# Rows of 256 columns without gaps for the moving operands of a two-block float32 network

## The chip, the cores and the metric

The kernel runs on one core of one Trainium2 chip. The metric is the device time of one execution in microseconds; lower is better. TensorE does the matrix products, ScalarE (ACT) and VectorE (DVE) split numbers and evaluate the elementwise parts, GpSimd (POOL) helps them, and SyncE (SP) issues nearly all the weight loads.

## The reference

Two blocks of depth 2 on a model width of 1024. The first block puts 16 meta tokens ahead of the 256 tokens of the sequence and works on 272 tokens; its result without the meta tokens goes to the second block.

```
first block, for each layer l of 2:
    h = h + 0.5 * swiglu(rmsnorm(h))                # 1024 -> 2 x 2816 -> 1024
    h = h + concat(retention(...), diff_attention(...)) @ w_out
    h = h + 0.5 * swiglu(rmsnorm(h))
h = rmsnorm(h)[:, 16:]
second block, for each layer i of 2:
    h = h + 0.5 * swiglu(rmsnorm(h))
    h = h + (short_conv if i == 0 else dilated_attention)(rmsnorm(h))
    h = h + 0.5 * swiglu(rmsnorm(h))
```

All data is float32, and so is the result.

## The kernel before

**Layout.** Everything is kept transposed: the model dimension lies on the 128 partitions in `KC` = 8 chunks, the tokens lie along the columns. `T` is 272 (16 meta tokens, `META`, and 256 tokens, `SEQ`). The residual `h` has rows of 272 columns for the whole kernel.

**Two parts for every number.** A float32 factor is split into a high part (rounded to the type fp32r) and a low part (the rest). A product of two such numbers takes three terms: high weights with the high input, high weights with the low input, low weights with the high input. The input of a stage is in `x[partition, chunk, part, column]`, the gated products of a feed-forward stage are in `a`, with 22 chunks (`FCH`) in place of 8, and the mixed values of an attention stage of the first block are in `y`. In all three a row has 272 columns, the high row of a chunk is followed by its low row, and the low row by the high row of the next chunk.

```
x = alloc(ctx, [P, KC, 2, T], F32R)
a = alloc(region, [P, FCH, 2, T], F32R)
y = alloc(region, [P, KC, 2, T], F32R)
```

**Stages.** `STAGES` lists twelve of them: feed-forward, mixer, feed-forward, feed-forward on all 272 tokens; a mixer (stage 4) whose keys and values need all 272 but whose queries and output need only the 256; and from there on 256 tokens alone: feed-forward (5), feed-forward (6), convolution (7), feed-forward (8), feed-forward (9), dilated attention (10), feed-forward (11). A stage of 256 tokens uses columns 16 to 271 of `x` and of `y`, and columns 0 to 255 of `a`. So it leaves a gap of 16 columns (64 bytes) between the rows that it reads.

**TensorE's loop.** One output tile is 128 channels by all tokens of the stage, summed in one PSUM bank over 8 chunks (22 in the down projection of a feed-forward stage, 2 tiles at a time). For each chunk and tile `matmuls` issues the three terms as three matmuls (lines 1641, 1642, 1643). In the five feed-forward stages of 256 tokens (`joined`) the first two terms are one matmul of 512 columns (line 1639), whose moving operand is `both(k)`: the high row and the low row of a chunk, two runs of 256 columns. Its sums with the high and the low rows lie side by side in one bank and are added later by ACT and DVE. The last two tiles of each down projection go back to three matmuls (`halves`). The text calls the matmuls of one chunk and tile, 768 columns in all, a *group*: two matmuls where the first two terms are joined, three elsewhere.

```
if both is not None:
    pe.matmul(ps[:, r.banks[j], :].rearrange("p (m n) -> p m n", m=2), hi, both(k), start=i == 0, stop=False)
else:
    pe.matmul(o, hi, xhi, start=i == 0, stop=False)
    pe.matmul(o, hi, xlo, start=False, stop=False)
ins = pe.matmul(o, lo, xhi, start=False, stop=i == r.nk - 1)
```

**Other buffers of 256 tokens.** The convolution keeps its result in `c_yy` and the dilated attention in `d_y`. Both are `[P, KC, 2, SEQ]` already, with rows of 256 columns without gaps, and their output projections read them with three matmuls a group. In the dilated attention the values are projected the other way round (`values`, lines 1959 to 1961): `x` is stationary there, and the moving operand is three pieces of 128 columns of the weights. The norms of queries and keys (lines 1894, 1895) move the rows `d_sqh` and `d_sql` of 512 columns in one run.

**Who feeds TensorE.** SP loads weights in pieces of up to 1 MB into a ring of four (`raw`), waiting for the low parts that DVE makes. ACT makes the high part of the weights (line 810), DVE the low part (line 1135), seven tiles ahead at most. ACT writes the high rows of `x` (823), `a` (909, 946) and `y`, DVE the low rows of `x` (1148), DVE or POOL those of `a` (1266, 743), POOL those of `y`. TensorE waits for the low row of each chunk (`xl`, `al`, `yl_d`, `yl_r`).

## Time and profile before

| | us |
|---|---|
| median of 3 runs (2184.85 to 2186.58) | 2186.07 |
| span of the profiled execution | 2188.4 |
| TensorE busy in the span | 2173.7 (99%) |
| VectorE busy | 1559.0 (71%) |
| ScalarE busy | 1221.3 (56%) |
| GpSimd busy | 438.6 (20%) |

The profiled execution is 2188.4 us long from its first to its last instruction, and no other time of it is given; it stands 2.3 us above the median of the runs. Matmuls are pipelined: the duration of one in the profile (281 ns for 256 columns) runs past the start of the next, so what a matmul costs in a dense stretch is the distance from its start to the next start. That distance is read from the timeline, over many groups, since its times are rounded to 10 ns. Some matmul records are missing from the trace, so distances are counted in groups by the order in the code, not by counting rows.

### The profile page before, as it was taken

To read this page: it belongs to the slowest core of one execution; us is meant where nothing else is said; L and a number is where in the kernel's file an instruction comes from. 1 tells how busy PE (TensorE), PEld (TensorE's weight loads), DVE (VectorE), ACT (ScalarE), POOL (GpSimd) and SP (SyncE) were. 2 spreads that over 40 slices of the span, in tenths; PEclk is the share of its full clock that TensorE was granted. 3 is DMA by queue.
4 is the path that set the end of the run, shared out by engine and by line. 5 is a ranking of instruction groups with operands and counts; after the bars stand their busy time and mean duration, and the time that the engine had idled before them with its cause. 6 is when DMAs were issued, how large, how long until landed. Compare 5 with 4: busy or idle time off the path is not lost.

```text
span 2188.4 us, 38657 instructions
## 1 busy us (share of the span) xinstructions
PE 2173.7 (99%) x15616; PEld 2045.6 (93%) x15616; DVE 1559.0 (71%) x2589; ACT 1221.3 (56%) x2020; POOL 438.6 (20%) x468
## 2 busy tenths in 40 slices
PE   9999999999999999999999999999999999999999
PEld 9999999999999999888988999889888999999888
DVE  7655876765665586876697587865876688887863
ACT  6444465544544446665565444655655566676652
POOL 1000522420350142231053000430331000000420
PEclk9999999999999999999999999999999999999999
DMA  8555434975786543565465554655555566674653
GB/s 271 195 171 177 155 122 136 232 199 167 196 209 179 169 154 116 173 205 185 162 204 198 196 182 146 221 198 186 185 185 179 160 190 168 176 236 140 222 177 104
DMA packets 429264, 395.34 MB, mean 181 GB/s; under 512 B 16559, under 2 KB 426031, under 8 KB 429088
## 3 DMA queue, kind: packets, MB, share of 16 engines
q1 hardware_dynamic: 416464, 377.11, 54.7%
q0 software_dynamic: 12336, 15.51, 3.6%
q8 instruction: 124, 2.03, 0.4%
q14 instruction: 52, 0.43, 0.1%
q10 hardware_dynamic: 288, 0.27, 0.0%
HBM read 389.20 MB, written 7.41 MB: 181 GB/s over the span
## 4 chain that ended last, share of the span: by engine, by line
PE 91%; DVE 4%; ACT 2%; DMA 1%; issue 1%; SPq 0%; DVEq 0%; ACTq 0%
PE ps L1643 29%; PE ps L1639 25%; PE ps L1641 16%; PE ps L1642 15%; DVE t L1135 2%; PE ps L1961 1%; PE ps L1960 1%; PE ps L1959 1%; DMA t<-attn_w_qkv 1%; ACT t L968 0%; PE ps L1927 0%; ACT t L810 0%; PE ps L1940 0%; PE ps L1911 0%; DVE t L1347 0%
## 5 line engine op out<-in xcount | busy, mean ns | idle before, releaser
L1643 PE MATMUL ps<-t 128*128 128x256 f32 (+1 forms) x5504 | 1563.6, 284 | 0.0
L1643 PEld LDWEIGHTS ps<-t 128*128 128x128 f32 x5504 | 1039.4, 189 | 0.1
L1135 DVE TENSOR_TENSOR t<-t 128x1024 fp32r<-128x1024 f32 (+1 forms) x724 | 880.5, 1232 | 176.5 <-ACT t L810 176.0
L1641 PE MATMUL ps<-t 128*128 128x272 f32 (+1 forms) x3084 | 891.9, 289 | 2.4 <-DVE t L1598 2.4
L1642 PE MATMUL ps<-t 128*128 128x272 f32 (+1 forms) x3084 | 883.6, 287 | 0.0
L810 ACT ACTIVATE t<-t 128x1024 fp32r<-128x1024 f32 (+1 forms) x724 | 731.9, 1030 | 263.3 <-PE ps L1643 235.1
L1639 PE MATMUL ps<-t 128*128 128x512 f32 x2420 | 847.4, 394 | 0.0
L1641 PEld LDWEIGHTS ps<-t 128*128 128x128 f32 x3084 | 582.5, 189 | 8.8 <-issue 5.0
L1642 PEld LDWEIGHTS ps<-t 128*128 128x128 f32 x3084 | 584.5, 190 | 0.9
L1639 PEld LDWEIGHTS ps<-t 128*128 128x128 f32 x2420 | 454.4, 188 | 103.3 <-DVE t L1135 0.3
L750 POOL TENSOR_TENSOR t<-t 128x256 f32<-128x256 f32 x110 | 100.9, 917 | 734.3 <-ACT t L926 734.3
L916 ACT ACTIVATE t<-ps 128x256 f32<-128x256 f32 x220 | 83.1, 378 | 138.7 <-PE ps L1643 138.3
L773 POOL DMA_DIRECT2D bias_bands<-bias_rows x128 | 105.1, 829 | 216.5 <-PE ps L1643 164.1
L743 POOL TENSOR_TENSOR t<-t 128x256 fp32r<-128x256 f32 x110 | 126.7, 1152 | 9.5 <-ACT t L909 9.5
L823 ACT ACTIVATE t<-t 128x256 fp32r<-128x256 f32 (+1 forms) x96 | 50.0, 531 | 93.5 <-DVE t L1220 83.5
L946 ACT ACTIVATE t<-t 128x272 fp32r<-128x272 f32 x66 | 28.5, 432 | 117.0 <-DVE t L1315 117.0
L1170 DVE SCALAR_TENSOR_TENSOR t<-ps,t 128x512 f32<-128x512 f32 (+2 forms) x52 | 28.6, 551 | 83.6 <-ACT t L851 83.2
L1281 DVE TENSOR_TENSOR t<-ps,t 128x256 f32<-128x256 f32 x110 | 46.7, 425 | 52.1 <-ACT t L916 49.3
L909 ACT ACTIVATE t<-t 128x256 fp32r<-128x256 f32 x110 | 45.4, 413 | 65.3 <-DVE t L1285 65.3
L1274 DVE TENSOR_TENSOR t<-ps,t 128x256 f32<-128x256 f32 x110 | 46.2, 420 | 47.6 <-ACT t L916 47.1
L1285 DVE TENSOR_TENSOR t<-t 128x256 f32<-128x256 f32 x110 | 69.3, 630 | 0.0
L1312 DVE TENSOR_TENSOR t<-ps,t 128x272 f32<-128x272 f32 x66 | 29.0, 440 | 51.0 <-PE ps L1643 51.0
(197 smaller groups left out, 1503.1 us busy)
## 6 DMA issues: line engine op xcount, KB each, us to landing
t<-ffn_w_in SPq DMA_DIRECT2D x88, 1024.0 KB, 5.3
t<-ffn_w_gate SPq DMA_DIRECT2D x42, 1024.0 KB, 5.4
t<-ffn_w_up SPq DMA_DIRECT2D x42, 1024.0 KB, 6.7
t<-attn_w_qkv SPq DMA_DIRECT2D x72, 512.0 KB, 4.9
t<-ffn_w_down SPq DMA_DIRECT2D x32, 1024.0 KB, 5.2
t<-ffn_w_out SPq DMA_DIRECT2D x32, 1024.0 KB, 5.2
t<-w_in SPq DMA_DIRECT2D x28, 1024.0 KB, 5.0
t<-ffn_w_down SPq DMA_DIRECT2D x16, 768.0 KB, 4.4
```

Source lines behind the costliest of these rows:

```text
L743: pool.tensor_tensor(a[:, j, 1, 0:SEQ], us[:, j % 2, 0:SEQ], f32(a[:, j, 0, 0:SEQ]), ALU.subtract).then_inc(S["al"], 1)
L750: pool.tensor_tensor(sl[:, j % 2, 0:SEQ], sl[:, j % 2, 0:SEQ], rstd[:, META:T], ALU.mult).then_inc(S["factor"], 1)
L773: pool.dma_start(bands.ap()[n, 64 * r:64 * r + 64, q, c:end].rearrange("i (k j) -> k i j", j=64), bass.AP(scr, n * NSEG * P + seg * P + 63 ...
L810: act.activation(whi[:, plan.place[n], 0:nk, :], raw[:, u % NRAW, 0:nk, half * P:half * P + P], ACT.Copy).then_inc(S["hi"], 1)
L823: act.activation(placed(e, x[:, m, 0, c0:T]), hm, ACT.Copy, scale=gain(e, m)).then_inc(S["xh"], 1)
L916: act.activation(part[:, m, :], ps[:, plan.bank[t], SEQ:2 * SEQ], ACT.Copy).then_inc(S["part"], 1)
L1135: dve.tensor_tensor(wlo[:, plan.place[n], 0:nk, :], raw[:, u % NRAW, 0:nk, half * P:half * P + P], f32(whi[:, plan.place[n], 0:nk, :]), AL ...
L1285: dve.tensor_tensor(us[:, i, 0:N], us[:, i, 0:N], sl[:, i, 0:N], ALU.mult).then_inc(S["prod"], 1)
L1639: pe.matmul(ps[:, r.banks[j], :].rearrange("p (m n) -> p m n", m=2), hi, both(k), start=i == 0, stop=False)
L1641: pe.matmul(o, hi, xhi, start=i == 0, stop=False)
L1642: pe.matmul(o, hi, xlo, start=False, stop=False)
L1643: ins = pe.matmul(o, lo, xhi, start=False, stop=i == r.nk - 1)
```

## The change

`close(t, n)` gives a second view of the same memory: the first `n * 512` columns of the buffer as `n` chunks of two rows of 256 columns. `x_close`, `a_close` and `y_close` are these views of `x`, `a` and `y`. `parts_of(e)` gives for the input of stage `e` the old view where it has 272 tokens and the new one where it has 256 (stages 5 to 11); `products_of(s)` and `mixed_of(s)` do the same for `a` and `y`. Stages 0 to 4 keep their input in the old view, and stage 4 has its mixed values in the new one. Everything that writes or reads these buffers goes through the three functions. The number of instructions, their order, their engines, their sizes and the semaphores are those of before. No buffer is added or made smaller.

```diff
--- before.py
+++ after.py
@@ -545,6 +545,25 @@
         def f32(ap):
             return ap.bitcast(F32)
 
+        def close(t, n):
+
+            whole = t[:, :, :, :].rearrange("p k m c -> p (k m c)")
+            return whole[:, 0:n * 2 * SEQ].rearrange("p (k m c) -> p k m c", k=n, m=2)
+
+        x_close, a_close, y_close = close(x, KC), close(a, FCH), close(y, KC)
+
+        def parts_of(e):
+
+            return x if start_of(e) == 0 else x_close
+
+        def products_of(s):
+
+            return a if STAGES[s][1] == 0 else a_close
+
+        def mixed_of(s):
+
+            return y if STAGES[s][1] == 0 else y_close
+
         def gain(e, m):
 
             if e == FINAL:
@@ -715,8 +734,8 @@
 
                 def low_y(kind, i, c):
                     w.wait_ge(*of_head("yh", l, kind, i))
-                    pool.tensor_tensor(y[:, c, 1, cq:T], yv[:, cq:T] if kind == "d" else qk[:, i, cq:T],
-                                       f32(y[:, c, 0, cq:T]), ALU.subtract).then_inc(S["yl_" + kind], 1)
+                    hi, lo = (mixed_of(s)[:, c, m, 0:T - cq] for m in range(2))
+                    pool.tensor_tensor(lo, yv[:, cq:T] if kind == "d" else qk[:, i, cq:T], f32(hi), ALU.subtract).then_inc(S["yl_" + kind], 1)
 
                 def step(what, i):
                     if what == "O2":
@@ -740,7 +759,7 @@
 
                 def low_a(j):
                     w.wait_ge(S["ah"], FCH * f + j + 1)
-                    pool.tensor_tensor(a[:, j, 1, 0:SEQ], us[:, j % 2, 0:SEQ], f32(a[:, j, 0, 0:SEQ]),
+                    pool.tensor_tensor(a_close[:, j, 1, :], us[:, j % 2, 0:SEQ], f32(a_close[:, j, 0, :]),
                                        ALU.subtract).then_inc(S["al"], 1)
 
                 w.wait_ge(S["rstd"], s + 1)
@@ -820,7 +839,7 @@
                 hm = residual(e, m, c0)
                 sem, value = made(e, m)
                 w.wait_ge(sem, value)
-                act.activation(placed(e, x[:, m, 0, c0:T]), hm, ACT.Copy, scale=gain(e, m)).then_inc(S["xh"], 1)
+                act.activation(placed(e, parts_of(e)[:, m, 0, 0:T - c0]), hm, ACT.Copy, scale=gain(e, m)).then_inc(S["xh"], 1)
 
             def squared(e, m):
                 c0 = start_of(e)
@@ -906,7 +925,7 @@
 
                 def high_a(j):
                     w.wait_ge(S["prod"], FCH * f + j + 1)
-                    act.activation(a[:, j, 0, 0:N], us[:, j % 2, 0:N], ACT.Copy).then_inc(S["ah"], 1)
+                    act.activation(products_of(s)[:, j, 0, 0:N], us[:, j % 2, 0:N], ACT.Copy).then_inc(S["ah"], 1)
 
                 def second(j, m, t):
 
@@ -943,7 +962,7 @@
                     act.activation(sl[:, j % 2, 0:N], gs[:, j % 2, 0:N], ACT.Silu).then_inc(S["silu"], 1)
                     behind(T0[s] + 2 * j)
                     w.wait_ge(S["prod"], n)
-                    act.activation(a[:, j, 0, 0:N], us[:, j % 2, 0:N], ACT.Copy).then_inc(S["ah"], 1)
+                    act.activation(products_of(s)[:, j, 0, 0:N], us[:, j % 2, 0:N], ACT.Copy).then_inc(S["ah"], 1)
                     behind(T0[s] + 2 * j + 1)
                 if joined(s)[0]:
                     high_a(FCH - 1)
@@ -988,7 +1007,7 @@
                     root(ps[:, bank, 0:NQ], lanes[lane][2][:, 0:NQ], lanes[lane][1][:, 0:NQ], "hroot_" + kind)
 
                 def high_y(kind, i, c):
-                    act.activation(y[:, c, 0, cq:T], yv[:, cq:T] if kind == "d" else qk[:, i, cq:T], ACT.Copy).then_inc(S["yh_" + kind], 1)
+                    act.activation(mixed_of(s)[:, c, 0, 0:NQ], yv[:, cq:T] if kind == "d" else qk[:, i, cq:T], ACT.Copy).then_inc(S["yh_" + kind], 1)
 
                 def step(what, i):
                     if what == "D1":
@@ -1145,8 +1164,8 @@
                 sem, value = made(e, m)
                 w.wait_ge(sem, value)
                 w.wait_ge(S["xh"], KC * e + m + 1)
-                dve.scalar_tensor_tensor(placed(e, x[:, m, 1, c0:T]), hm, gain(e, m), placed(e, f32(x[:, m, 0, c0:T])),
-                                         ALU.mult, ALU.subtract).then_inc(S["xl"], 1)
+                hi, lo = (parts_of(e)[:, m, i, 0:T - c0] for i in range(2))
+                dve.scalar_tensor_tensor(placed(e, lo), hm, gain(e, m), placed(e, f32(hi)), ALU.mult, ALU.subtract).then_inc(S["xl"], 1)
 
             def added(e, m):
                 c0 = start_of(e)
@@ -1263,7 +1282,7 @@
 
                 def low_a(j):
                     w.wait_ge(S["ah"], FCH * f + j + 1)
-                    dve.tensor_tensor(a[:, j, 1, 0:N], us[:, j % 2, 0:N], f32(a[:, j, 0, 0:N]),
+                    dve.tensor_tensor(products_of(s)[:, j, 1, 0:N], us[:, j % 2, 0:N], f32(products_of(s)[:, j, 0, 0:N]),
                                       ALU.subtract).then_inc(S["al"], 1)
 
                 def both_parts(j, n, t, i):
@@ -1650,8 +1669,9 @@
                     if r.piece == 0:
 
                         w.wait_ge(*((S["lo_first"], k + 1) if k < KC - 1 else (S["lo"], 4)))
-                matmuls(r, range(KC), lambda k, c0: (x[:, k, 0, c0:T], x[:, k, 1, c0:T]), ready, hook,
-                        both=(lambda k: x[:, k, :, META:T]) if STAGES[r.stage][0] == FFN and joined(r.stage)[0] else None)
+                xs, first = parts_of(r.stage), start_of(r.stage)
+                matmuls(r, range(KC), lambda k, c0: (xs[:, k, 0, c0 - first:T - first], xs[:, k, 1, c0 - first:T - first]), ready, hook,
+                        both=(lambda k: x_close[:, k, :, :]) if STAGES[r.stage][0] == FFN and joined(r.stage)[0] else None)
 
             def norm(e):
                 c0 = start_of(e)
@@ -1699,8 +1719,8 @@
                     w.wait_ge(S["al"], FCH * f + k + 1)
                 for r in runs:
                     if r.first - T0[s] >= 2 * FCH:
-                        matmuls(r, range(FCH), lambda k, c0: (a[:, k, 0, 0:N], a[:, k, 1, 0:N]), ready,
-                                both=(lambda k: a[:, k, :, 0:N]) if halves(s, r) else None)
+                        matmuls(r, range(FCH), lambda k, c0: (products_of(s)[:, k, 0, 0:N], products_of(s)[:, k, 1, 0:N]), ready,
+                                both=(lambda k: a_close[:, k, :, :]) if halves(s, r) else None)
 
             def start_work():
                 w.wait_ge(S["squares"], 64)
@@ -1862,7 +1882,7 @@
                         w.wait_ge(*of_head("hn", l, "r", 3))
                     if m in (6, 7):
                         w.wait_ge(*of_head("hn", l, "d", 3))
-                    matmuls(r, OUT_ORDER, lambda k, c0: (y[:, k, 0, c0:T], y[:, k, 1, c0:T]), ready, each=each if m == 0 else None)
+                    matmuls(r, OUT_ORDER, lambda k, c0: (mixed_of(s)[:, k, 0, 0:NQ], mixed_of(s)[:, k, 1, 0:NQ]), ready, each=each if m == 0 else None)
 
             def conv(s):
                 runs = plan.runs[s]
@@ -1954,7 +1974,7 @@
                         w.wait_ge(S["evac"], plan.earlier[r.first + j] + 1)
                         for k in range(KC):
                             hook[j](k)
-                            xhi, xlo = (x[:, k, m, META + j * P:META + (j + 1) * P] for m in range(2))
+                            xhi, xlo = (x_close[:, k, m, j * P:(j + 1) * P] for m in range(2))
                             hi, lo = (wt[:, p0:p0 + 3, k, :] for wt in (whi, wlo))
                             pe.matmul(o, xhi, hi, start=k == 0, stop=False)
                             pe.matmul(o, xhi, lo, start=False, stop=False)
```

## Rows read from the trace of the kernel before

**Rows 1.** The page: engines, clock in 40 slices, chain that ended last.

```profile
PE 2173.7 (99%) x15616; PEld 2045.6 (93%) x15616; DVE 1559.0 (71%) x2589; ACT 1221.3 (56%) x2020; POOL 438.6 (20%) x468
...
PEclk9999999999999999999999999999999999999999
...
PE 91%; DVE 4%; ACT 2%; DMA 1%; issue 1%; SPq 0%; DVEq 0%; ACTq 0%
```

**Rows 2.** Waits of TensorE: engine line, for whom, us in total, times, longest.

```profile
PE ps L1940 <- ACT t L1082: 2.6, 1, 2.6
PE ps L1641 <- DVE t L1598: 2.4, 2, 1.9
```

**Rows 3.** Busy time by stretch: window, us, then each engine; last clock, DMA share, GB/s.

```profile
1100.00:1200.00 100.00, 100.00 (x574) 87.84 (x573) 84.90 (x123) 62.59 (x115) 45.02 (x40) 1.00 0.64 211
1275.00:1330.00 55.00, 55.00 (x466) 55.00 (x465) 48.73 (x84) 23.19 (x28) 0.00 (x0) 1.00 0.64 212
1790.00:1940.00 150.00, 150.00 (x1316) 144.36 (x1315) 126.53 (x228) 108.83 (x170) 4.75 (x9) 1.00 0.68 190
```

**Rows 4.** Groups by line and form, TensorE: count | busy us, mean ns | idle.

```profile
L1643 PE MATMUL ps<-t 128*128 128x256 f32 x3504 | 985.7, 281 | 0.0
L1639 PE MATMUL ps<-t 128*128 128x512 f32 x2420 | 847.4, 394 | 0.0
...
L1641 PE MATMUL ps<-t 128*128 128x256 f32 x1084 | 308.7, 285 | 0.0
```

**Rows 5.** Timeline, TensorE, up projection of stage 5: start us, duration us.

```profile
1001.18 0.39 PE L1639 MATMUL ps<-t 128*128 128x512 f32 x1
1001.42 0.28 PE L1643 MATMUL ps<-t 128*128 128x256 f32 x1
...
1008.88 0.39 PE L1639 MATMUL ps<-t 128*128 128x512 f32 x1
```

**Rows 6.** Timeline, TensorE, down projection of stage 6, joined groups.

```profile
1230.26 0.39 PE L1639 MATMUL ps<-t 128*128 128x512 f32 x1
...
1237.92 0.39 PE L1639 MATMUL ps<-t 128*128 128x512 f32 x1
```

**Rows 7.** Timeline, TensorE, down projection of stage 6, last two tiles.

```profile
1254.90 0.29 PE L1641 MATMUL ps<-t 128*128 128x256 f32 x1
...
1263.76 0.28 PE L1641 MATMUL ps<-t 128*128 128x256 f32 x1
```

**Rows 8.** Timeline, TensorE, projections of stage 7 from `x`.

```profile
1299.97 0.28 PE L1641 MATMUL ps<-t 128*128 128x256 f32 x1
...
1300.33 0.28 PE L1641 MATMUL ps<-t 128*128 128x256 f32 x1
...
1300.68 0.28 PE L1641 MATMUL ps<-t 128*128 128x256 f32 x1
...
1307.81 0.28 PE L1641 MATMUL ps<-t 128*128 128x256 f32 x1
```

**Rows 9.** Timeline, TensorE, output projection of stage 7 from `c_yy`.

```profile
1337.90 0.28 PE L1641 MATMUL ps<-t 128*128 128x256 f32 x1
...
1344.90 0.28 PE L1641 MATMUL ps<-t 128*128 128x256 f32 x1
```

**Rows 10.** Timeline, TensorE, projections of stage 10 from `x`.

```profile
1819.03 0.28 PE L1641 MATMUL ps<-t 128*128 128x256 f32 x1
...
1824.01 0.28 PE L1641 MATMUL ps<-t 128*128 128x256 f32 x1
```

**Rows 11.** Timeline, TensorE, values and norms of stage 10.

```profile
1837.92 0.39 PE L1894 MATMUL ps<-t 128*128 128x512 f32 x1
1838.15 0.39 PE L1895 MATMUL ps<-t 128*128 128x512 f32 x1
1838.38 0.34 PE L1959 MATMUL ps<-t 128*128 128x384 f32 x1
...
1843.07 0.40 PE L1894 MATMUL ps<-t 128*128 128x512 f32 x1
```

## The prediction, made before the changed kernel was run

> **What bounds the kernel now.** I read the page first: TensorE is busy for 99% of the span, its clock is granted in full in all 40 slices, and 91% of the chain that ended last is TensorE's own [rows 1]. Then TensorE's waits: the longest is 2.6 us, the next 2.4 us in sum [rows 2], so nothing feeds it late. Then stretches inside the stages that the change touches: in a feed-forward stage, the convolution and the dilated attention TensorE is never idle, the clock is 1.00, and the next engine, DVE, is busy for 84.9, 88.6 and 84.4% [rows 3]. The kernel's time is the sum of the distances between matmul starts. The change adds and removes no instruction. It can change the time only if these distances depend on where the rows of the moving operand lie. That is the one question, and the timeline answers part of it.
>
> **The distances now.** All are of a group: one chunk, one tile, 768 columns.
> - Joined, from `x`: 22 groups between 1001.18 and 1008.88, so 350.0 ns [rows 5].
> - Joined, from `a`: 22 groups between 1230.26 and 1237.92, so 348.2 ns [rows 6].
> - Three matmuls, from `a`: 25 groups between 1254.90 and 1263.76, so 354.4 ns [rows 7].
> - Three matmuls, from `x`, convolution: 22 groups between 1299.97 and 1307.81, so 356.4 ns. They alternate between about 0.36 and 0.35 us, with even and odd chunks [rows 8].
> - The same in the dilated attention: 14 groups between 1819.03 and 1824.01, so 355.7 ns [rows 10].
> - Three matmuls from `c_yy`, whose rows have no gaps: 20 groups between 1337.90 and 1344.90, so 350.0 ns [rows 9].
>
> The last two kinds differ in nothing but the buffer: same three terms, same 256 columns, same clock, same engine busy without a pause. With gaps a group costs 6.4 ns (1.8%) more than without. That the distance alternates with the parity of the chunk fits: with gaps a chunk is 2176 bytes, so the starting place of its rows within any larger block of memory differs from chunk to chunk, and in `c_yy`, at 2048 bytes a chunk, it does not.
>
> **What the groups become.** The number of groups follows from the loops and agrees with the counts by form [rows 4]. Up projections: 5 stages x 44 tiles x 8 chunks = 1760 joined groups. Down projections: 5 x 6 x 22 = 660 joined (together the 2420 of line 1639) and 5 x 2 x 22 = 220 of three matmuls. Convolution: 24 x 8 = 192. Dilated attention, queries and keys: 48 x 8 = 384. Output of stage 4: 8 x 8 = 64. The remaining 224 of the 1084 groups of line 1641 are the output projections from `c_yy` and `d_y` (128) and the queries and gates of stage 4 (96), whose `x` stays as it is.
>
> Groups of three matmuls: the nearest row is `c_yy`, and I take its 350.0 ns. That gives 220 x 4.4 = 1.0 us, 192 x 6.4 = 1.2 us, 384 x 5.7 = 2.2 us, and for the 64 of stage 4, which I cost like those from `a`, 64 x 4.4 = 0.3 us. Sum 4.7 us. Bounds: nothing (the address has another effect than I think), and the 4.7 us in full plus as much again as 348 ns instead of 350 would give, 860 x 2 = 1.7 us, so 6.4 us.
>
> Joined groups: no row shows 512 columns of a joined group without the gap. Three rows are near. The values of the dilated attention move 384 columns of the weights in runs that have no odd offsets: 27 matmuls in the 4.69 us between 1838.38 and 1843.07, so 173.7 ns each, 0.452 ns per column [rows 11]. `c_yy` gives 116.7 / 256 = 0.456 ns. The norms move 512 columns in one run: two distances, 0.46 us together, 230 ns or 0.449 ns per column [rows 11]; these were short stretches, read to 10 ns. For 768 columns this makes 347.4, 350.0 and 345.0 ns. The joined groups from `a` stand at 348.2 already, though they have the gap, so part of what a gap costs is gone where two rows are read in one instruction. I take 348.0 ns for both kinds: 1760 x 2.0 = 3.5 us and 660 x 0.2 = 0.1 us. Bounds: nothing if they stay as they are, and with 345.0 ns, 1760 x 5.0 + 660 x 3.2 = 10.9 us.
>
> **A rule weighed.** Rows 11 and 5 show 0.23 us for 512 columns in one run and 0.24 us for 512 in two runs with a gap between. The Trainium skill (Advanced Engine Details and Errata, Memory Cachelines) says that any non-contiguous access pattern slows down matmuls significantly; it says so of PSUM, and if it held for the moving operand too, joining two runs into one would be worth much more than my 3.6 us. The trace doesn't bear this out: by the two rows the difference is 10 ns at most, and by the groups 5 ns.
>
> **The rest of the change at nothing.** ACT, DVE and POOL write the same numbers of elements into rows that start elsewhere, with unit steps as before. These writes lie beside TensorE, which waits for none of them now, and in the tightest stretch, the convolution, DVE still has 11% of its time free [rows 3]. If TensorE gets 1.8% faster there, DVE's share goes from 88.6 to 90.2%, and it stays covered. Were the cover gone, the cost would be the lateness of `xl` or `al` at a chunk, of which there is none now beyond [rows 2]. The values in stage 10 only load their stationary operand from the new view; the moving one is the weights, so their 173.7 ns stay. No buffer is shared by two stages at once in a new way: the input of a stage is written after the projections of the one before are done, and no wait is added. Transfers follow DVE and find the same ring, and they are busy for 0.64 to 0.68 of the time [rows 3]; 0.4% more is no strain.
>
> **The sum.** 4.7 + 3.6 = 8.3 us of the profiled 2188.4, so a span near 2180.1. The profile stands 2.3 us above the median of the runs, and the saving is the same there: 2186.1 - 8.3 = 2177.8 us, 0.38% faster. About 0.2%, 4.4 us, is what a measurement of this kernel can tell from no change.
>
> **The rivals.**
> - *Only groups of three gain.* The joined ones read two rows in one instruction, and the gap between them may cost nothing, as the 350.0 of `x` joined equals the 350.0 of `c_yy`. Against it stands `a` joined at 348.2 with another start of its rows: the start matters in joined groups too. Time 2186.1 - 4.7 = 2181.4.
> - *Nothing changes.* The 6.4 ns of the convolution would then come from something else that differs between its projections and its output, such as DVE and ACT, which work harder in the projections. For it: I have compared stretches, not the same stretch twice. Against it: the distances repeat with the parity of the chunk, which the work of DVE doesn't. Time 2186.1. The Trainium skill (TensorE: Matmul & The Clock Gate, Back-to-back issue gap) gives columns / 2.4 GHz + 2.5 ns from start to start, in which no address stands; by that rule a joined group is 325 ns now and after. The trace has 350, so the rule lacks the very part that is in question here.
> - *The joined groups gain all that the bound allows*: 2186.1 - 4.7 - 10.9 = 2170.5.
> - *Slower: every row starts at the bad place.* In the convolution groups of one parity take about 0.35 and of the other 0.36 us [rows 8]; as 356.4 is their mean, the slow ones take some 362 ns if the fast ones take what `c_yy` does. After the change all chunks of `x` and of `a` start at the same place within 1024 bytes, and high and low rows too. If this is the slow one, every group takes 362 ns: 1760 x 12 + 660 x 13.8 + 220 x 7.6 + 576 x 6.2 + 64 x 7.6 = 35.9 us more, 2222 us. It decides as soon as the changed groups average above the present mean, which is (1760 x 350.0 + 660 x 348.2 + 284 x 354.4 + 576 x 355.9) / 3280 = 351.1 ns. Against it: `c_yy`, `d_sqh` and the weights as moving operand, three buffers with equal starts for all rows, are all at or under 350.
>
> **How the numbers follow.** Forecast (both kinds gain, 6 to 12 us) 0.55; only groups of three 0.15; nothing 0.17; the largest gain 0.05; slower 0.08. Predicted 2177.8. The range leaves out the slower case and the far end of the largest gain: 2171.0 to 2186.3. The forecast's own range is 2174 to 2180. Faster by over 0.2%: 0.55 + 0.05, and 0.08 of the second case, which lies on the bound: 0.68. Within 0.2%: 0.17 + 0.07 = 0.24. Slower: 0.08.
>
> **What would show it.** In the timeline after, the projections of the convolution no longer alternate, and 22 groups take 7.70 us instead of 7.84 (step one). In the up projections 22 groups take 7.66 instead of 7.70, and 7.59 at the bound (step two). The down projections keep 7.66. The output of the convolution keeps 350.0. Stages 0 to 3 take the same time to within a microsecond. The waits of TensorE are as short as before. The prediction is wrong if the convolution stays at 356 (then the address was not the cause), or if the up projections rise above 351 ns a group.

## The result and the profile after

| | before | after |
|---|---|---|
| median of 9 runs each, us | 2185.34 (2183.92 to 2186.58) | 2188.70 (2186.32 to 2194.17) |
| span of the profiled execution | 2188.4 | 2187.9 |

The ratio is 1.0018, with a 95% interval of 1.0010 to 1.0025: the changed kernel is slower by 0.18%, which is within the 0.2% that the prediction called no change. The forecast was 2177.8 us, and the measured time lies above its range. The runs after lie 7.9 us apart, those before 2.7; but on the chip of the first experiments 15 runs of the kernel before lay 6.5 us apart (2184.21 to 2190.71), so such a spread is no mark of the change.

The page after (engines, chain), and TensorE's longest waits:

```profile
PE 2176.6 (99%) x15616; PEld 2043.4 (93%) x15616; DVE 1557.4 (71%) x2589; ACT 1222.2 (56%) x2020; POOL 441.5 (20%) x468
...
PE 93%; DVE 3%; ACT 2%; DMA 1%; issue 1%; SPq 0%; DVEq 0%; ACTq 0%
```

```profile
PE ps L1914 <- DVE t L1523: 2.0, 2, 1.1
PE ps L1960 <- ACT t L1101: 1.4, 1, 1.4
PE ps L1792 <- ACT t L1026: 1.4, 2, 0.8
```

As in [rows 1, 2] TensorE is the bound and hardly waits. So the answer is again in the distances. Timeline of TensorE after (start us, duration us), each pair of rows 22 groups apart: first the up projections of stage 5, then those of stage 6, then the last two tiles of stage 6's down projection, then the projections of the convolution from `x`:

```profile
950.26 0.40 PE L1658 MATMUL ps<-t 128*128 128x512 f32 x1
...
957.88 0.40 PE L1658 MATMUL ps<-t 128*128 128x512 f32 x1
...
1100.15 0.40 PE L1658 MATMUL ps<-t 128*128 128x512 f32 x1
...
1107.93 0.40 PE L1658 MATMUL ps<-t 128*128 128x512 f32 x1
...
1250.20 0.28 PE L1660 MATMUL ps<-t 128*128 128x256 f32 x1
...
1258.12 0.28 PE L1660 MATMUL ps<-t 128*128 128x256 f32 x1
...
1290.02 0.28 PE L1660 MATMUL ps<-t 128*128 128x256 f32 x1
...
1297.94 0.28 PE L1660 MATMUL ps<-t 128*128 128x256 f32 x1
```

Divided by 22 these are 346.4, 353.6, 360.0 and 360.0 ns a group, against 350.0 [rows 5], 354.4 [rows 7] and 356.4 [rows 8]. The groups of three from `x` and `a` are slower than before, and at exactly 120 ns a matmul they no longer alternate between chunks. The joined groups do what no step of the prediction allows for: with the same rows at the same places, stage 5 runs at 346.6 and stage 6 at 353.4. The means over the groups of a stage in the two traces, in ns (distances between neighbouring groups with no other matmul and no wait between them; in stages 7 and 10 the projections from `x`, in stage 4 the output from `y`), and how long each stage lasts, from its first norm matmul to the next stage's, in us:

| stage | 4 | 5 | 6 | 7 | 8 | 9 | 10 | 11 |
|---|---|---|---|---|---|---|---|---|
| joined, before | | 349.6 | 349.6 | | 349.6 | 349.6 | | 349.6 |
| joined, after | | 346.7 | 353.4 | | 347.1 | 353.3 | | 353.4 |
| of three, before | 355.2 | 354.9 | 354.9 | 356.1 | 354.9 | 354.9 | 355.5 | 354.9 |
| of three, after | 350.4 | 359.7 | 360.0 | 359.9 | 359.7 | 360.0 | 359.4 | 360.0 |
| lasts, before | 141.9 | 182.1 | 185.6 | 94.1 | 182.1 | 180.9 | 289.5 | 176.6 |
| lasts, after | 140.9 | 181.1 | 187.7 | 95.0 | 181.1 | 182.9 | 288.3 | 178.5 |

Stages 4 to 11 together last 2.6 us longer after. Stages 5 and 8 gain 1.0 us each, and 6, 9 and 11 lose 2.1, 2.0 and 1.9, each as its groups say (stage 6: 484 x 3.8 + 44 x 5.1 = 2.1 us). Stage 4 gains 0.3 us in its output, whose groups from `y` fell from 355.2 to 350.4 ns, and 0.5 in shorter waits. Stage 10 loses 1.5 us in its groups: once it is in its steady course, a pair of heads takes 31.69 us in place of 31.50. That it is 1.2 us shorter all the same has two causes that have nothing to do with its groups: its longest wait fell from 2.6 to 1.4 us, and in the trace of the kernel before TensorE had half its clock for 3.4 us, right behind that wait. Window, us, engines, then clock (0.50 is 1.2 GHz, 1.00 is 2.4), in the kernel before:

```profile
1764.00:1767.00 3.00, 0.37 (x5) 0.17 (x4) 1.45 (x2) 2.54 (x4) 0.00 (x0) 1.00 0.96 254
1767.40:1770.80 3.40, 3.40 (x31) 2.81 (x26) 2.28 (x4) 3.34 (x6) 0.00 (x0) 0.50 0.82 236
```

An estimate from its length and clock is that it costs 1.7 us, so at the full clock stages 4 to 11 would last 4.3 us longer after. Two more lie in stage 0 (from 12.96 and from 67.57 us, 3.4 us each), and the trace after has none: its mean granted clock is 1.000, against 0.998 before. That is why stages 0 to 3, which the change leaves alone, took 3.1 us less in it, and why the profiled span after is shorter than the one before. The medians of nine runs are the measure.

### The profile page after: what moved, and what is told of

It is laid out like the page before. It is cut to its first block, busy times and chain, and to the rows that moved or that the text cites. A ratio compares the mean times of both kernels' runs of the same rounds, so it can differ in the third digit from the quotient of the medians.

```text
span 2187.9 us, 38657 instructions
## 1 busy us (share of the span) xinstructions
PE 2176.6 (99%) x15616; PEld 2043.4 (93%) x15616; DVE 1557.4 (71%) x2589; ACT 1222.2 (56%) x2020; POOL 441.5 (20%) x468
## 4 chain that ended last, share of the span: by engine, by line
PE 93%; DVE 3%; ACT 2%; DMA 1%; issue 1%; SPq 0%; DVEq 0%; ACTq 0%
PE ps L1662 29%; PE ps L1658 26%; PE ps L1660 16%; PE ps L1661 16%; DVE t L1154 1%; PE ps L1981 1%; PE ps L1979 1%; PE ps L1980 1%; DMA t<-attn_w_qkv 1%; PE ps L1947 0%; ACT t L829 0%; PE ps L1931 0%; PE ps L1960 0%; PE ps L1757 0%; ACT t L866 0%
```

## The experiments

Two theories stood at the outset. *Address*: the distance is a function of where the rows start. *Rhythm*: rows that all start alike let the stream of matmuls fall into one of several self-repeating patterns, and one layout has several distances. A third was traffic of the other engines. All ratios are to the kernel before, run on the same chip; differences between two changed kernels in microseconds can be across chips.

**1. Streams of groups alone** (m1_streams). A kernel of its own, 1475.7 us long: no gating, no evacuation, nothing but matmuls in 32 stretches after the operands are loaded.

```
for seg, (kind, first, stride, low, tiles, pause) in enumerate(SEGMENTS):
    ...
    hi, lo = whi[:, n % NP, k, :], wlo[:, n % NP, k, :]
    ...
        pe.matmul(o, hi, xh, start=k == 0, stop=False)
        pe.matmul(o, hi, xl, start=False, stop=False)
    pe.matmul(o, lo, xh, start=False, stop=k == KC - 1)
```

> This kernel computes nothing of the reference: it loads four weight pieces, splits them, copies the input to both rows of x, and then runs 32 stretches of the group's matmuls with no other engine at work, most after a short pause; its output is the untouched input. It varies the layout of the moving rows (with gaps as in x and in a; without; without and shifted by 8, 16, 32 columns; gap only between chunks; gap only between high and low row), the kind of group (two or three matmuls), and what ran just ahead. Address theory (the distance is a function of where the rows start): each layout has one distance wherever it stands, three matmuls without gaps 359.8 ns, joined without gaps 347 or 353, and shifts of 8 to 32 columns move it. Rhythm theory (equal rows let the stream fall into one of several self-repeating rhythms, which lasts until something breaks it): the same joined stretch without gaps takes 346.7 in some places and 353.3 in others, depending on whether three-matmul groups or a pause came ahead; with gaps 350 always. Traffic theory (DVE, ACT or DMA traffic makes the difference): with these idle, all layouts take the same, near 347.

Its timeline, 22 groups apart: groups of three without gaps at a shift of 0, at a shift of 16 columns, then joined groups without gaps at a shift of 0 in two of the stretches:

```profile
130.31 0.28 PE L112 MATMUL ps<-t 128*128 128x256 f32 x1
...
138.23 0.28 PE L112 MATMUL ps<-t 128*128 128x256 f32 x1
...
225.05 0.28 PE L112 MATMUL ps<-t 128*128 128x256 f32 x1
...
232.53 0.28 PE L112 MATMUL ps<-t 128*128 128x256 f32 x1
...
400.31 0.40 PE L110 MATMUL ps<-t 128*128 128x512 f32 x1
...
408.08 0.40 PE L110 MATMUL ps<-t 128*128 128x512 f32 x1
...
1070.23 0.39 PE L110 MATMUL ps<-t 128*128 128x512 f32 x1
...
1077.85 0.39 PE L110 MATMUL ps<-t 128*128 128x512 f32 x1
```

360.0, 340.0, 353.2 and 346.4 ns. The traffic theory falls: with the other engines idle the stretches give the kernel's own numbers (gaps as in `x`: 356.7 of three, 350.0 joined; gaps as in `a`: 355.0 of three; no gaps: 360.0 of three). One number differs: joined groups with gaps as in `a` take 350.0 here and 348.4 in the kernel, whose down projection takes two tiles in turn; that difference isn't explained. The places matter, and by more than the prediction had thought: 16 columns (64 bytes) of shift are worth 20 ns a group in this run. And for joined groups the rhythm theory holds as well: the same layout ran at 353.3 in five stretches and at 346.7 in three. The five had no or one small matmul ahead of them, the three had two, three and four.

**2. The curve over the shift** (m2_starts), in the same kind of kernel, 1151.5 us.

> Again streams of groups alone, computing nothing of the reference, 38 stretches of 80 groups: groups of three matmuls of 256 columns without gaps whose rows all start 0, 2, 4, ... 80 columns past a place divisible by 1024 bytes; two in which only the high or only the low row is shifted by 16; joined groups at other shifts; and rows of 272 columns in five pitches. In the run before, shifts of 0, 8, 16 and 32 columns gave 360.0, 350.0, 340.0 and 356 ns. If the start within some block of memory sets the distance, the curve over the shift is smooth or stepped and repeats with a period, and 80 columns equal one of the smaller shifts. If only the high row's place counts (it is read twice), the mixed stretches stand near their high row's value. If the distance depends on the relation to the rows of the weights, which start at multiples of 512 bytes, the period is at most 128 columns. Rival: the four values were chance rhythms; then neighbours of a shift show no order and a repeated shift of 0 or 16 gives another value.

Groups of three, rows of 256 columns without gaps, ns by shift in columns (with what runs 1 and 3 add):

```
shift   0    2    4    6    8        12   14   16       18   20   24   28   32   40   48       56   64   80
ns     360  360  356  360  350/353  355  360  340/353  360  355  360  340  356  352  340/353  355  360  353
```

0 and 64 agree, and so do 16 and 80, while 32 and 48 differ from 0 and 16: as far as these two pairs show, the curve repeats at 64 columns (256 bytes). It isn't smooth. 16 gave 340.0 in the first run and 353.3 in this one, so groups of three have rhythms too. With only the low rows shifted by 16 the groups take 353.3, with only the high rows 356.7. Joined groups never fell under 346.7 at any shift.

**3. The rhythms, and the place of the weights** (m3_rhythms), 1121.6 us.

> Streams of groups alone once more, 38 stretches, computing nothing of the reference. Five stretches each of three-matmul groups without gaps at shifts of 28, 48 and 16 columns after different pauses; the same right after joined groups; ten in which the rows of the weights are shifted too; and rows of 272 columns in other pitches. So far 28 and 48 gave 340.0 once each, 16 gave 340.0 once and 353.3 once, 0 and 64 gave 360.0 each time. Address theory in its strict form: 28 and 48 give 340.0 five times of five, and 16 is an outlier to be explained. Rhythm theory: 28 and 48 too show other values after other pauses, and 0 is special only in that all its rhythms cost 360. If what counts is where the moving row starts relative to the row of the weights, moving 0 with weights 28 or 36 runs at 340 to 356 and moving 28 with weights 28 at 360; if the weights do not matter, moving 0 stays at 360.0 and 28 at 340.0 whatever the weights' shift.

A shift of 28 gave 340.0 six times of six, 16 gave 353.3 five times of five, 48 gave 340.0 three times and 353.3 three times, depending on what ran ahead (one or three small matmuls: 340.0; two, four, or joined groups: 353.3). Then the rows of the weights were shifted. Timeline, 22 groups apart: moving rows at 0 and weights at 16, then both at 16:

```profile
760.18 0.28 PE L102 MATMUL ps<-t 128*128 128x256 f32 x1
...
767.66 0.28 PE L102 MATMUL ps<-t 128*128 128x256 f32 x1
...
790.06 0.28 PE L102 MATMUL ps<-t 128*128 128x256 f32 x1
...
797.98 0.28 PE L102 MATMUL ps<-t 128*128 128x256 f32 x1
```

340.0 and 360.0: the moving row at 0 is not slow by itself; it is slow against a weight row at the same place within 256 bytes. Pairs of (moving, weights) at (0, 0), (16, 16), (48, 48) and (64, 64) all took 360.0, (0, 48) took the 353.3 of a shift of 16. For shifts that are no multiple of 16 columns the difference is not the whole story: (28, 28) took 355.0, not 360, and (0, 36) took 360.0, not the 340 of a shift of 28; (0, 28) took 360.0 too.

**4. The changed kernel once more** (e1_again, a single run, 2188.7 us).

> The changed kernel, unchanged, profiled once more, on another chip perhaps. Address theory: joined groups of stages 5 and 8 again at 347.1 ns and those of 6, 9 and 11 at 353.4. Rhythm theory, if the rhythm is entered by chance: some stages swap, and the span moves by about 3.2 us (484 groups x 6.6 ns) for each; if it is set by what runs ahead: the same pattern.

Stages 5, 6, 8 and 9 kept their distances; stage 11 ran at 346.7 in place of 353.3 (22 groups from 2100.33 to 2107.96 us). So a stage can swap from one execution to the next, by some 3 us (450 groups x 6.7 ns). Part of the spread of the runs after may come from that, but no trace was taken of one of the longest; another part goes with the granted clock, which is 0.998 in the two slowest of the 15 runs of the kernel before and 0.999 to 1.000 in the others.

**5. All tiles of the down projection joined** (e2_all_joined).

```diff
-            return STAGES[s][0] == FFN and joined(s)[0] and r.first + r.n < T0[s + 1]
+            return STAGES[s][0] == FFN and joined(s)[0] and r.first >= T0[s + 1] - KC
```

> The changed kernel with the last two tiles of each down projection joined too, so the five feed-forward stages of 256 tokens hold no group of three matmuls. Rhythm theory: without the groups of three (359.8 ns) between stages 5 and 6 and stages 8 and 9 nothing pushes the next stage into the slow rhythm; stages 6 and 9 run at 347, 484 groups x 6.4 ns x 2 = 6.2 us, and the 220 groups themselves save 13 ns each, 2.9 us: 2188.7 - 9 = 2180 us. Address theory: the joined groups stay as they are, and only the 220 change: 2188.7 - 220 x 6.4 to 13 ns = 2186 to 2187 us.

2185.8 us, ratio 0.9997 (0.9988 to 1.0006). A miss for the 2180 expected: stage 6 went over to 346.7, but stage 9 ran at 353.3, though no group of three runs between 8 and 9 any more. The trace shows where it changed. Stage 9 in this run, 22 groups, then its norm matmuls (L1683, one pair of 256 columns in the middle of the projections), then 22 groups again:

```profile
1526.03 0.39 PE L1658 MATMUL ps<-t 128*128 128x512 f32 x1
...
1533.65 0.39 PE L1658 MATMUL ps<-t 128*128 128x512 f32 x1
...
1534.01 0.40 PE L1683 MATMUL ps<-t 128*128 128x256 f32 x2
...
1536.00 0.40 PE L1658 MATMUL ps<-t 128*128 128x512 f32 x1
...
1543.78 0.40 PE L1658 MATMUL ps<-t 128*128 128x512 f32 x1
```

346.4 ns ahead of the norm, 353.6 behind it. Without the groups of three stages 6 and 9 did take over the 346.7 of the stage before; stage 6 kept it through its norm matmuls, stage 9 lost it there. The same holds in the other traces: stage 8 of the changed kernel went from 353 to 346.7 at its norm, and so did stage 11 of e1_again. In the 400 and more groups behind its norm matmuls no feed-forward stage whose rows have no gaps changed its rhythm in any trace, as long as the kind of group stayed the same. So a rhythm changes where something breaks the stream, and which one follows isn't set by the last two tiles alone.

**6. A shift of 48 columns** (e3_shift48), and **three matmuls everywhere with a shift of 48 or 28** (e4_plain48, e5_plain28).

```diff
-            return whole[:, 0:n * 2 * SEQ].rearrange("p (k m c) -> p k m c", k=n, m=2)
+            return whole[:, SHIFT:SHIFT + n * 2 * SEQ].rearrange("p (k m c) -> p k m c", k=n, m=2)
...
-            return STAGES[s][1] == META, FCH * (ffn_of[s] - 3)
+            return False, 0
```

The first hunk is the shift, the second gives up the joined matmul. With it POOL's share of those stages goes back to DVE (a third hunk, not shown, takes it out of POOL's program), and DVE takes the gate and up tiles straight from PSUM.

> The changed kernel with its views of 256 columns starting 48 columns further into the buffers, which adds nothing else. Address theory, with the values of the streams alone: groups of three at 340 in place of 359.8 (576 of x, 220 of a, 796 x 20 = 16 us), joined groups at 353.3 in place of the present mix of 347 and 353 (at most 2640 x 6.6 = 17 us lost, about 8 if one counts the stages that already run at 353): 2188.7 - 16 + 8 = 2181 us. If shifts do not matter in the kernel: 2188.7 us.

> As the run before, and the joined matmul given up: the five feed-forward stages of 256 tokens go the way of the stages of 272 tokens, three matmuls a group, with the gate and up tiles evacuated by DVE straight from PSUM and no work of POOL. Address theory: all 3280 groups at 340: 351.1 - 340 = 11 ns x 3280 = 36 us under the kernel before, 2150 us, if DVE keeps up. Rhythm theory: the rhythm of 340 isn't kept everywhere, and stages differ; anything from 2150 to 2200 us.

> The same with a shift of 28 columns in place of 48. Both 28 and 48 ran at 340.0 alone, so the address theory gives the same 2150 us for both; a difference between them by stage would show that in the kernel, with the other engines at work, more than the start of the row decides.

The shift alone: 2189.2 us, ratio 1.0015 (1.0005 to 1.0024), 8 us above what was expected. The projections from `x` fell to 341.7 and 343.6 ns, which is worth 7 us against the kernel before; but all joined groups took 353.3 (2420 x 3.7 = 9 us lost) and those of three from `a` 353.3 instead of 340. With three matmuls everywhere: 2161.0 us for 48, ratio 0.9882 (0.9867 to 0.9897), and 2156.4 us for 28, ratio 0.9867 (0.9851 to 0.9884). In the traces all feed-forward stages with 28 ran at 340.0 to 340.3. With 48 stage 6 went from 340.0 to 353.3 at its norm matmuls and stayed there; stages 5 and 11 went from 353.3 to 340.0 at theirs, and 8 and 9 ran at 340. That is the picture of the streams: 28 keeps one rhythm, 48 has two. Both stayed above the 2150 expected. With 28 the groups explain some 3 of the 6 us: the projections of the dilated attention ran at 343.5, and the output of stage 4, whose `y` isn't at the place of `x`, at 354.9. The rest isn't explained.

**7. Which of the two did it** (p0_plain, p0_weights16, p_gaps). No shift; no shift but the weights moved; and the gaps of before; all with three matmuls everywhere. What the second changes in the first:

```diff
+        alloc(ctx, [P, 16])
         whi = alloc(ctx, [P, NP, 8, P], F32R)
         wlo = alloc(ctx, [P, NP, 8, P], F32R)
+        alloc(ctx, [P, 48])
```

> The changed kernel with the joined matmul given up (three matmuls a group in all stages) and no shift: rows of 256 columns that all start at a place divisible by 256 bytes, as the rows of the weights do. Address theory: every one of the 3280 groups at 360, so 3280 x (360 - 351.1) = 29 us above the kernel before, about 2215 us. If giving up the joined matmul is what made the two kernels with shifts fast, this one is fast as well, near 2156 us.

> The kernel just named, with one thing moved: the two buffers of the weights start 16 columns (64 bytes) later, by an unused strip ahead of them, and a strip of 48 columns behind them puts every other buffer back to its place within 256 bytes. No moving row has another place than in the kernel with 2215 us expected. If the place of the moving row by itself decides, the time is that one's, 2215 us. If the place of the moving row against the row of the weights decides, the groups run at 340 as they did alone with this pair of starts, 3280 x 20 = 66 us less, near 2150 us; 353 in some stages is possible, as with a shift of 48, which is the same difference.

> The kernel before, with gaps, with the joined matmul given up and nothing else. From the streams alone: groups of x at 356.7 in place of 350.0 (1760 x 6.7 = 11.8 us), groups of a at 355.0 in place of 348.3 (660 x 6.7 = 4.4 us): 2185.7 + 16 = 2202 us. If it is fast instead, the two kernels with shifts owe their time to giving up the joined matmul, and not to the places of the rows.

| | us | ratio, interval | expected |
|---|---|---|---|
| no gaps, no shift | 2213.4 | 1.0128 (1.0113 to 1.0143) | 2215 |
| the same, weights moved by 64 bytes | 2155.5 | 0.9859 (0.9844 to 0.9874) | 2150 |
| gaps | 2201.9 | 1.0071 (1.0056 to 1.0086) | 2202 |

Timeline of the up projections of stage 5, 22 groups apart, in the first and in the second kernel:

```profile
950.15 0.28 PE L1657 MATMUL ps<-t 128*128 128x256 f32 x1
...
958.07 0.28 PE L1657 MATMUL ps<-t 128*128 128x256 f32 x1
```

```profile
950.01 0.28 PE L1659 MATMUL ps<-t 128*128 128x256 f32 x1
...
957.49 0.28 PE L1659 MATMUL ps<-t 128*128 128x256 f32 x1
```

360.0 and 340.0. Nothing but two unused strips lies between 2213.4 and 2155.5 us: 64 bytes ahead of the weights and 192 behind them, so that every buffer behind moves by 256 bytes and keeps its place within 256. Stage 11 of the second kernel went from 340 to 353.3 at its norm matmuls, some 490 groups x 13.3 ns = 6.5 us, which covers the 5 us above what was expected. Giving up the joined matmul is no gain by itself: it costs 15.7 us with gaps and 24.7 us without (2213.4 against the 2188.7 of the changed kernel, which ran on another chip).

The buffers that no edit touches bear this out. The output projection of the convolution reads `c_yy`, which has the same place in all these kernels. It took 350.0 ns a group in the kernel before, and in the changed kernel, 22 groups:

```profile
1324.55 0.28 PE L1660 MATMUL ps<-t 128*128 128x256 f32 x1
...
1332.33 0.28 PE L1660 MATMUL ps<-t 128*128 128x256 f32 x1
```

**8. The stages of 272 tokens shifted too** (p28_all).

```diff
-        x = alloc(ctx, [P, KC, 2, T], F32R)
+        x = alloc(ctx, [P, KC * 2 * T + 64], F32R)[:, 28:28 + KC * 2 * T].rearrange("p (k m c) -> p k m c", k=KC, m=2)
...
-                a = alloc(region, [P, FCH, 2, T], F32R)
+                a = alloc(region, [P, FCH * 2 * T + 64], F32R)[:, 28:28 + FCH * 2 * T].rearrange(
+                    "p (k m c) -> p k m c", k=FCH, m=2)
```

> The kernel with the shift of 28 columns and three matmuls everywhere, with the stages of 272 tokens shifted by 28 columns too (buffers of x and a longer by 64 columns, so that all others keep their places within 256 bytes). Alone, rows of 272 columns in the present pitch took 372.3 ns with a shift of 28 and 376.7 without. Address theory: stages 0, 2 and 3 with 528 groups each and the 448 projections of stages 1 and 4 from x save 4.4 ns, 2032 x 4.4 = 8.9 us: 2156.4 - 9 = 2147.5 us. Otherwise 2156 us.

2148.6 us, ratio 0.9829 (0.9812 to 0.9845). The groups of stages 0, 2 and 3 fell from 376.6 to about 373 ns, here 22 groups of stage 2:

```profile
400.21 0.28 PE L1660 MATMUL ps<-t 128*128 128x272 f32 x1
...
408.41 0.28 PE L1660 MATMUL ps<-t 128*128 128x272 f32 x1
```

This is the best version found: 37.6 us under the kernel before and 40 under the changed one.

## Why the prediction was wrong, by its own steps

- **What bounds the kernel**: right. TensorE's distances are the time, before and after; the waits stayed short, and DVE, ACT, POOL and the transfers stayed covered. One reading was too strong: the digit 9 stands for 90% or more, so "granted in full in all 40 slices" isn't what [rows 1] says. The trace before had three stretches of 3.4 us at half the clock, by the estimate above some 5 us in all of the 2188.4 us that the sum starts from.
- **"The last two kinds differ in nothing but the buffer ... With gaps a group costs 6.4 ns more than without"**: this is the step that failed. The rows were read rightly, and `x` with gaps and `c_yy` without differ by the buffer; but buffers differ in more than their gaps, namely in where their rows start against the rows of the weights. The gap as such costs nothing fixed: without gaps the same group takes anything from 340 to 360 ns (experiments 1 and 2), and with gaps, where the starts vary from chunk to chunk, 355 to 357, as a mean over several places would. `c_yy` happened to lie at a place worth 350.0 or 353.3 ns, `x` and `a` at the worst (experiment 7). The row of 350.0 wasn't even a fixed price of `c_yy`: after the change it took 353.4, where the prediction has it keep 350.0. The alternation with the parity of the chunk was the right clue, that the start counts; it was taken as a sign that even starts are good, when it only says that starts differ.
- **Groups of three at 350.0**: from `x` and `a` measured 359.4 to 360.0, so 4.4 us of gain became 3.3 us of loss (220 x 5.0 + 192 x 3.8 + 384 x 3.9). The 64 from `y` did go to 350.4 and gained the 0.3 us, by the luck of where `y` lies.
- **Joined groups at 348.0**: measured 350.8 as a mean, against 349.6 before, and no stage had 350.8 or 348.0. Two ran at 346.7 and 347.1 and gained 2.6 us, as the step had it in kind; three ran at 353.3 to 353.4 and lost 5.5. That one layout can have two distances was in no step and no rival. The bound "nothing, if they stay as they are" was therefore no bound.
- **The slower rival, "every row starts at the bad place"**: it named the mechanism and nearly its size, 362 ns for groups of three against 360.0 measured. It was given 0.08 because `c_yy`, `d_sqh` and the weights as moving operand seemed three witnesses for equal starts. They were witnesses for their own places only. It erred in letting joined groups pay the same, 12 to 14 ns; they pay 3.3 from `x` and 5.0 from `a` at worst. p0_plain, where all groups are of three, is this rival in pure form: 2213.4 us.
- **"Nothing changes"** came closest in time, for another reason than it gave: losses of 9.0 us and gains of 2.9 in the groups, and some 2 us less of waits, which together leave 4 us. That so little is left of them is luck.
- **The rule on non-contiguous patterns** was weighed rightly. Joined groups with the gap take 350.0 in the streams, without it 346.7 or 353.3; a shift of 64 bytes without any gap counts for more than the gap.

What the experiments show, then, for these fp32r matmuls: TensorE's distance depends on where the moving rows start and where the weight rows start, and for starts at multiples of 64 bytes on the difference of the two, within 256 bytes. The Trainium skill (SBUF — State Buffer, Who interferes with whom; TensorE: Matmul & The Clock Gate, Step-by-step: what each phase is for) says that the moving operand and the weights are read through two independent ports, and that loading weights takes no read bandwidth from a running matmul. The pair of kernels in experiment 7 doesn't fit that: with the moving rows at the same places within 256 bytes and the weights moved by 64 bytes, the time changes by 2.6%; nor does the pair of streams in experiment 3, 340.0 against 360.0 ns.

Open are two things. Why the curve over the shift has the values it has, in particular for shifts that are no multiple of 64 bytes, isn't explained. And what decides which of its rhythms a stretch falls into isn't settled. It changes only where something breaks the stream: a different number of matmuls ahead of it (experiment 1), groups of another kind, or the norm matmuls in the middle of a stage (experiment 5). Which rhythm follows can differ between two executions of one kernel, as in stage 11 (experiment 4). That the rhythm persists through a stage is measured; that it is the work of a collision between two read streams that repeats is an inference.

## What to carry to other kernels

Where TensorE is the bound and busy all the time, read the distance between matmul starts and compare it with columns divided by the clock; here 768 columns are 320 ns at 2.4 GHz, and the kernel paid 350. If there is an excess, try the place of the operands before their shape: a strip of unused columns ahead of the weights, or a shift of the moving buffer, is a line or two. With three matmuls everywhere it was worth 2.6% here, from the worst place to a good one, and the best version lies 1.7% under the kernel before; with the joined matmul kept, a shift of 48 columns was worth nothing. Don't lay moving rows and weight rows at the same place within 256 bytes, and don't take a row from another buffer as the price of a layout without asking what else differs about that buffer.

A trick that saves instructions (the joined matmul) was right for the places of before, 15.7 us, and wrong for good places, where three matmuls take 340.0 and the joined pair never got under 346.7: with a shift of 48 columns giving it up gained 28 us (2189.2 to 2161.0). And compare layouts by more than one trace, since one layout can have two distances.

## What was not expected of the hardware

- Most stretches of groups of three run at 340.0, 350.0, 353.3, 355.0, 356.7 or 360.0 ns, to a tenth of a nanosecond over some 80 groups. These are multiples of 1.67 ns, four cycles of the 2.4 GHz clock, which suggests patterns that repeat exactly. A few stretches (352.0 and 356.0 ns) are not.
- The same stretch can stay in a rhythm of 346.7 or of 353.3 for 160 us, through its evacuations and its weight loads by DMA, with a neighbour of the same code in the other. It changes at an interruption as short as one pair of norm matmuls.
- Moving the weights by 64 bytes changed a kernel of 2.2 ms by 57.9 us.
